# Attention's output projection: remainders of the early tiles ahead of the whole tiles, combinations in that order, first weights' high part sooner

## The reference

```python
def diff_attn(...):
    ...
    o = _rms_f32(o, g_sub) * (1.0 - lambda_init)
    o = o.transpose(0, 2, 1, 3).reshape(B, L, D_V_W).astype(xn.dtype)
    return o @ w_out

def swiglu(xn, w_in, w_out):
    gu = xn @ w_in
    g = gu[..., :FF]
    u = gu[..., FF:]
    return (jax.nn.silu(g) * u) @ w_out

def trunk(...):
    ...
            h = h + diff_attn(...)
        xn = rmsnorm(h, norm_ffn[i])
        h = h + swiglu(xn, ffn_w_in[i], ffn_w_out[i])
    return h[:, N_META:]
```

## Time and profile before

| | |
|---|---|
| median of 3 runs | 1980.11 us (1978.26 to 1980.32) |
| the profiled execution | 1979.85 us |
| its span | 1978.0 us |
| PE busy | 1931.5 us, 98% |
| DVE busy | 1138.6 us, 58% |
| ACT busy | 723.7 us, 37% |
| POOL busy | 1093.0 us, 55% |

### The profile page before, as it was taken

One profiled execution on the slowest core, in us unless ns is written; L12 is line 12 of the kernel. 1 busy time (PEld: TensorE's weight loads), 2 busy tenths in 40 slices (PEclk: granted clock), 3 DMA queues, 4 the chain that ended last, 5 costly groups with the idle time before them and its releaser, 6 DMA issues.

```text
span 1978.0 us, 30306 instructions
## 1 busy us (share of the span) xinstructions
PE 1931.5 (98%) x11129; PEld 1802.3 (91%) x11129; DVE 1138.6 (58%) x1928; ACT 723.7 (37%) x1447; POOL 1093.0 (55%) x1503
## 2 busy tenths in 40 slices
PE   8999999999999999999999999999989999999998
PEld 7898988899999999999978888888888898998997
DVE  7756464777365264266566666666685562562651
ACT  5333333445143142143224444445452340440531
POOL 4532323358596596596622222222467894984973
PEclk9999999999999999999999999999989999999999
DMA  4111111212221221222211111101211222222213
GB/s 158 43 33 40 46 32 33 77 48 59 70 86 55 68 70 56 73 65 71 66 43 33 33 32 32 32 27 38 59 43 57 83 64 71 69 70 59 81 55 95
DMA packets 214920, 114.90 MB, mean 58 GB/s; under 512 B 7011, under 2 KB 213510, under 8 KB 214550
## 3 DMA queue, kind: packets, MB, share of 16 engines
q1 hardware_dynamic: 212816, 112.62, 19.4%
q10 hardware_dynamic: 1990, 0.76, 0.2%
HBM read 108.57 MB, written 4.78 MB: 57 GB/s over the span
## 4 chain that ended last, share of the span: by engine, by line
PE 83%; DVE 6%; POOL 5%; ACT 2%; issue 2%; DMA 2%; ACTq 0%; DVEq 0%; SPq 0%; POOLq 0%
PE ps L625 44%; PE ps L679 25%; POOL wl L555 3%; PE ps L847 3%; PE ps L1008 2%; PE ps L976 2%; POOL wxl L555 2%; PE ps L827 1%; DMA raw<-in_ffn_w_in_dram 1%; PE ps L998 1%; PE ps L910 1%; PE ps L856 0%; DVE raw L1235 0%; PE ps L940 0%; ACT wh L1943 0%
## 5 line engine op out<-in xcount | busy, mean ns | idle before, releaser
L544 POOL CAST wh<-raw 128x256 fp32r<-128x256 f32 x428 | 165.6, 427 | 747.3 <-PE ps L625 710.9
L679 PE MATMUL ps<-sx,wh 128*128 128x400 f32 (+1 forms) x1408 | 368.3, 343 | 7.9 <-POOL wl L555 6.5
L555 POOL TENSOR_TENSOR wl<-raw,wh 128x256 fp32r<-128x256 f32 x352 | 319.2, 936 | 89.7 <-ACT wh L1943 89.4
L548 POOL TENSOR_TENSOR wl<-raw,wh 128x256 fp32r<-128x256 f32 x428 | 333.9, 809 | 10.4
L679 PE MATMUL ps<-sx,wxh 128*128 128x400 f32 (+1 forms) x1056 | 275.8, 342 | 10.5 <-ACT u L1950 8.8
L679 PEld LDWEIGHTS ps<-sx,wh 128*128 128x128 f32 x1408 | 259.2, 189 | 9.0 <-issue 6.8
L679 PE MATMUL ps<-sx,wl 128*128 128x400 f32 (+1 forms) x704 | 241.1, 342 | 0.0
L1943 ACT ACTIVATE wh<-raw 128x512 fp32r<-128x512 f32 x176 | 106.7, 628 | 365.2 <-PE ps L625 239.7
L555 POOL TENSOR_TENSOR wxl<-raw,wxh 128x256 fp32r<-128x256 f32 x220 | 223.7, 1042 | 12.8 <-ACT wxh L1943 12.8
L625 PE MATMUL ps<-xh,wh 128*128 128x400 f32 (+2 forms) x768 | 221.9, 365 | 0.0
L625 PE MATMUL ps<-xl,wh 128*128 128x400 f32 (+2 forms) x768 | 213.2, 351 | 0.0
(11 more groups left out here) (265 smaller groups left out, 3343.5 us busy)
## 6 DMA issues: line engine op xcount, KB each, us to landing
raw<-in_ffn_w_in_dram SPq DMA_DIRECT2D x154, 256.0 KB, 3.0
raw<-in_ffn_w_out_dram SPq DMA_DIRECT2D x48, 384.0 KB, 3.5
raw<-in_m_w_in_dram SPq DMA_DIRECT2D x24, 512.0 KB, 3.8
raw<-in_d_w_in_dram SPq DMA_DIRECT2D x24, 512.0 KB, 3.9
rawx<-in_ffn_w_in_dram SPq DMA_DIRECT2D x22, 256.0 KB, 3.0
raw<-in_m_w_out_dram SPq DMA_DIRECT2D x8, 512.0 KB, 4.1
raw<-in_ffn_w_out_dram SPq DMA_DIRECT2D x16, 256.0 KB, 2.7
wk<-in_x_prompt_dram SPq DMA_DIRECT2D x4, 512.0 KB, 5.8
```

The lines of the kernel that those rows point to most:

```text
L544: ins = pool.tensor_copy(wh[:, slot, c], raw[:, slot, c])
L548: ins = pool.tensor_tensor(wl[:, slot, c], raw[:, slot, c], wh[:, slot, c].bitcast(F32), ALU.subtract)
L555: ins = pool.tensor_tensor(slot_of(j, 1)[:, c], factor(g, j)[:, c], slot_of(j, 0)[:, c].bitcast(F32), ALU.subtract)
L679: mm = pe.matmul(product_bank(g, j, layer), slot_of(j, low_w)[:, k * P:(k + 1) * P], sx[layer][:, k * NPROD + j, low_x, :], start=(j in OP ...
```

## The change

Four things are moved, none added or removed.

- PE: behind the first seven k-steps of `whole(0)` and two of `whole(1)`, the four remainders come first, then what is left of the two whole tiles. The second pair of remainders goes to the banks that the first pair used, and so waits for DVE's adds of the first pair.
- DVE: the adds into h follow that order, and the combinations take the pairs 0, 2, 1, 3 (before 1, 0, 2, 3).
- POOL's splits of LATE[2] and LATE[3] keep their place, but wait for the blocks of the whole tiles, which now count later.
- ACT: the high part of the first weights (product 0) is made in the third combination behind xo, no longer behind its last square.

```diff
-PAIR_ORDER = ((0, 1, 2, 3), (1, 0, 2, 3))
+REST_END, WHOLE_END, LATE_END = OUT1 + 4, OUT1 + 6, OUT1 + 8
+PAIR_ORDER = ((0, 1, 2, 3), (0, 2, 1, 3))
...
             for q in range(2):
-                pool.wait_ge(block_done, WHOLE1 + q + 1)
+                pool.wait_ge(block_done, WHOLE_END + q + 1)
                 split(REST1 + 2 + q, q, REST1 // 2 + 2, wait=False)
...
-            pe.wait_ge(acc_free, WHOLE1)
+            pe.wait_ge(acc_free, OUT1 + 4)
             whole(1, 3, k1=2)
             pe.wait_ge(yl_ready, YL_AT[OUT1])
+            rest(0, 0, 2)
+            rest(0, 1, 1)
+            pe.wait_ge(rest_added, 1)
+            rest(1, 0, 2)
+            pe.wait_ge(acc_free, REST_END + 1)
+            rest(1, 1, 1)
             whole(0, 0, k0=7)
             whole(1, 3, k0=2)
-            rest(0, 0, 2)
-            rest(0, 1, 1)
-            pe.wait_ge(acc_free, WHOLE1 + 1)
-            rest(1, 0, 0)
-            pe.wait_ge(acc_free, WHOLE1 + 2)
-            rest(1, 1, 3)
-            pe.wait_ge(rest_added, 1)
+            pe.wait_ge(rest_added, 2)
             run_block(REST1 + 2, 0, 2, (yh, yl), tokens="packed", free=False)
-            pe.wait_ge(acc_free, REST1 + 1)
+            pe.wait_ge(acc_free, REST_END + 2)
             run_block(REST1 + 3, 1, 1, (yh, yl), tokens="packed", free=False)
...
                 elif at == 0:
-                    add_tile(WHOLE1, LATE[0], 0)
+                    add_rest(0, 2)
...
                 elif at == 0:
-                    add_tile(WHOLE1 + 1, LATE[1], 3)
+                    add_tile(REST_END, EARLY[1], 1)
                 elif last:
-                    add_tile(REST1 + 3, LATE[3], 1)
+                    add_tile(LATE_END + 1, LATE[3], 1)
...
-                if layer == 1 and at < 2:
-                    add_rest(at, *((2, 1), (0, 3))[at])
+                if layer == 1 and at == 0:
+                    add_rest(1, 2)
+                    add_tile(REST_END + 1, EARLY[3], 1)
+                elif layer == 1 and at == 1:
+                    add_tile(WHOLE_END, LATE[0], 0)
+                    add_tile(WHOLE_END + 1, LATE[1], 3)
                 elif layer == 1 and at == 2:
-                    add_tile(REST1 + 2, LATE[2], 2)
+                    add_tile(LATE_END, LATE[2], 2)
                     sum_1(g)
...
                 with_gain(2 * k + 1, xo)
                 if last:
                     weight_high(g, 3, next_n0, g)
+                if layer == 1 and at == KP - 2:
+                    weight_high(g, 0, next_n0, g)
...
                 square(2 * k + 1, 2 * at + 1)
                 if layer == 1 and at == KP - 2:
-                    weight_high(g, 0, next_n0, g)
                     weight_high(g, 1, next_n0, g)
```

More of the change, by code:

```diff
@@ L1198, in add_tile, with add_rest @@
                 add_packed(h[:, m, :], p).then_inc(acc_free, 1)
-            def add_rest(q, p0, p1):
+            def add_rest(q, p):
                 ve.wait_ge(rest_done, q + 1)
-                add_packed(h[:, EARLY[2 * q], :], p0).then_inc(rest_added, 1)
-                add_tile(REST1 + q, EARLY[2 * q + 1], p1)
+                add_packed(h[:, EARLY[2 * q], :], p).then_inc(rest_added, 1)
             def out_blocks(n0, norm, gain_at):
@@ L1935, in weight_high @@
                     if g:
-                        sc.wait_ge(block_done, REST1 + 2)
+                        sc.wait_ge(block_done, REST_END + 2)
                 if j in (0, 3):
@@ L1968, in tile_complete @@
                     else:
-                        n = {LATE[0]: WHOLE1, LATE[1]: WHOLE1 + 1, EARLY[1]: REST1, EARLY[3]: REST1 + 1,
-                             LATE[2]: REST1 + 2, LATE[3]: REST1 + 3}[m]
+                        n = {LATE[0]: WHOLE_END, LATE[1]: WHOLE_END + 1, EARLY[1]: REST_END, EARLY[3]: REST_END + 1,
+                             LATE[2]: LATE_END, LATE[3]: LATE_END + 1}[m]
                         sc.wait_ge(acc_free, n + 1)
```

## The result

The changed kernel takes 1983.67 us (median of 14 runs, 1981.11 to 1985.82), the kernel before, measured beside it, 1980.21 (14 runs). The ratio is 1.0017, 95% interval 1.0009 to 1.0024: slower by 0.17%, inside the 0.2% that I took as the limit of what can be told, but a real 3.5 us where I had forecast 1.3 to 1.5.

A forecast was written before the change was run, and what follows sets the result against it. The prediction took the start of product 2, set by the chain of four combinations on DVE and ACT, as what counts. Its terms summed to +1.5 us there, on a profiled 1979.85: 1981.4 us, range 1977.8 to 1984.6.

The forecast's parts named there:

- the upper bound of the contention: At product 2: every moved POOL subtraction costs one chain operation 0.51 us, only old costs given back; +3.7 us, 1983.6.
- rival B: PE's clock falls in the last wait before product 2, over some 5 us at half deciding; 3 us lost, 1984.4; chance 0.12.
- Start: First combination's start: DVE's first add +1.5 us, but its wait before the next add drops out; net +0.2 us.
- From tx2 to the adds: First combination on DVE, tx2 to adds: POOL is now idle there, 2.65 us becomes 2.10; -0.55 us.
- First tail: First combination, adds to running sum: LATE[2]'s split meets three DVE operations, replacing 0.6 us of old contention; +0.9 us.
- Second combination: LATE[3]'s split meets four DVE operations there, two on the chain (running sum, tx2); +1.0 us.
- Weights' pass: Third combination: first weights' high part made sooner saves 0.57 us, but POOL's split meets two lows; net +0.45 us.
- fourth combination: POOL has one split instead of two there, freeing one of DVE's two lows; -0.5 us.
- Projection 2.5 later: Attention's output projection on PE ends about 2.5 us later, covered since DVE needs the last tile near 1448; no cost.
- My other sign of B: Clock under 1.00 after product 2, with no catching up by 1505, would show the forecast wrong.
- A: POOL's moved splits miss DVE's operations, running in its waits; chain moves -0.5 to -2.5 us, about 1978.4; chance 0.27.
- C: First add's delay not recovered, or a block waits for LATE[2]'s split; first term +1.5 instead of +0.2, 1982.7; chance 0.08.

The follow-up runs named there:

- e6: Kernel before plus four matmuls with unread results in the projection, so that it ends 2.57 us later: 1980.52 us, ratio 1.0005.
- e3: Changed kernel, weights' pass in its old place, LATE[2] split by POOL ahead of the remainders in buffers of its own, LATE[3] into slot 0: 1981.86 us, 1.0013.
- e5: Kernel before with POOL's four subtractions for LATE[3] done twice, same values: 1982.21 us, ratio 1.0010.
- e8: Kernel before with LATE[2] split ahead of the remainders, LATE[3] right behind them, each into own slots, and the weights' pass sooner: 1979.94 us, 0.9995.
- e2: Kernel before with only the first weights' high part moved sooner: 1979.38 us, ratio 0.9998.
- e4: Changed kernel with PE's three waits ahead of product 2 filled with matmuls whose results nobody reads: 1980.88 us, ratio 1.0007.
- e1: Changed kernel with the first weights' high part back in its old place, so the reordering alone: 1983.37 us, ratio 1.0017.
- e7: Kernel before with LATE[2] split ahead of the remainders and LATE[3] from shared raw buffer 1 into slot 0: 1980.46 us, ratio 1.0004.
- e9: Changed kernel with the early splits of e8 for LATE[2] and LATE[3]: 1982.54 us, ratio 1.0010.
- e10: e8 with PE's three waits filled as in e4 (1, 5 and 5 matmuls): 1978.93 us, ratio 0.9994.

## Why the prediction was right, and where its size was not

The sign and "within 0.2%" held. The median lies in the range, near its upper end; it owes that to the room that the range left for the upper bound of the contention and for rival B, since the size itself was 3.5 where I had 1.3 to 1.5. The argument (the chain through DVE and ACT counts, not the projection or product 0) was right: e6 moved the projection's end for nothing, e3 and e5 moved product 2 through POOL alone, and in e8 product 0 started 5 us sooner while product 2 came 1.44 sooner. Term by term, at product 2:

- **Start, +0.2: measured -0.02.** DVE's first two adds came 4.78 and 9.39 us after POOL's first cast, where I had 4.65 and 9.6, and the second without a wait, as said.
- **From tx2 to the adds, -0.55: -0.55.**
- **First tail, +0.9: +1.11.** LATE[2]'s split began where I put it (14.08 after POOL's first cast; I had 14.0) and met three low parts, as I had it, and then the running sum, too (1.52 in place of 0.98).
- **Second combination, +1.0: +2.15. This is the mis-sized term.** I wrote that LATE[3]'s split meets four operations of DVE, two of them on the chain, and that xe "hides behind ACT's high part". I had given the split about 5 us. It lasted 6.98 (1424.34 to 1431.32), because DVE holds POOL up as well: its casts took 2.50 for four in place of 1.43, its subtractions 4.40 in place of 2.83. So it reached eight operations: three at 0.75, five (the running sum, tx2, xe and both low parts) at 1.08 to 1.09. And at 1 us each, DVE has no wait left between them: ACT is ahead, and what had hidden is on the chain.
- **Weights' pass, +0.45: +0.32**, and **fourth combination, -0.5: -0.61.** Their difference, -0.29, agrees with e2's -0.31 by itself.
- **Projection 2.5 later, at nothing: 2.41 later, nothing** (e6).
- Sum: +2.4 in place of +1.5.

Of the second combination's 2.15, 1.95 lie between tx2 and the adds: 4.05 us in place of 2.10. There tx2 costs 0.53 more, xe 0.33, and the two low parts, which my count of the chain left out, 1.09. The running sum, which I had counted, cost nothing: from its start to tx2's it is 1.01 in both kernels (1426.60 to 1427.61 above, 1425.28 to 1426.29 before). The other 0.20 lie ahead of it. The line of before:

```profile
1425.28 0.99 DVE L1252 TENSOR_TENSOR tsum<-tsum,tsq 128x800 f32<-128x800 f32 x1 [0.21 <-ACT tsq L1988]
```

**Rival B came in part.** I priced it at 3 us, to be added if the clock fell in the wait ahead of product 2, and gave it 0.12. It did fall, though not in that wait: it fell within product 0, behind the first of the three waits, and stayed at half through the other two and into product 2, for some 3 us of it, below the 5 us that I had set as deciding. PE lost 1.5 us by it, and 0.7 were still there near 1505, by e4; the next waits took up the rest. My other sign of B, no catching up by 1505, came true for those 0.7. The measured terms plus this are 3.1 at PE near 1505, against 3.5 in the medians; the last 0.4 are within the runs' scatter, and no run parts them. Rivals A and C did not come: POOL's new places met DVE at its densest, and PE waited for no split of LATE[2] or LATE[3].

**The Trainium skill's rule** (SBUF — State Buffer, "Who interferes with whom"), that the port pair which VectorE and GpSimd share is an exclusive lock, would have given +3.5 by my estimate. The measured sum, +2.4, stands between it and mine, and the rows are nearer to the rule than I allowed: from start to start, a DVE operation takes 0.47 alone and a POOL subtraction 0.71; where both are dense, each DVE operation takes 1.01 and each subtraction 1.1, so that a pair takes nearly the sum of the two, 1.18. I had read the price off DVE's side alone (0.51 an operation) and left out that POOL pays as well.

## What to carry to other kernels

When work of one engine slows another, the slowed pair must be laid out in time for both: POOL's split beside a dense DVE is not its old length moved, it took 6.98 us in place of 4.4 undisturbed, and reached operations that a count with its old length left out; a step that "hides" behind a third engine hides only as long as its own engine has waits. Before moving work to a later place, look for an earlier one: the splits, of which one alone cost 2.1 us where it was pushed back (e3 against e1), gave 1.1 when they were pulled ahead (e8, less the pass's 0.3), and that needed a buffer of their own (e8), since a shared one put them right back (e7). A late end on an engine whose next work waits for another chain costs nothing (e6), but splitting one long wait into several moved the clock's fall and its recovery (back at 1450.6 before, near 1458.8 changed), and that can land under the work that counts.

## What the runs showed of the hardware that I had not expected

- DVE and POOL slow each other, DVE by 0.54 an operation and POOL by 0.39 a subtraction where both are dense: from start to start, DVE's 128x384 fp32 operations take 0.47, 0.67 beside POOL's casts of 128x256 and 1.01 beside its subtractions; four casts of POOL go from 1.43 to 2.50, four subtractions from 2.83 to 4.40. DVE's adds from PSUM are not slowed (1.93 to 1.94 for four in every profile).
- The clock need not fall within a wait. It fell 2.5 us into the wait of 6.54 (before), but 1.4 us behind the end of one of 2.82 (changed), 0.3 us behind one of 2.34 (e9) and 0.5 us behind one of 4.63, which passed at full clock (e3). At the wait near 1571, of 2.4 to 2.6 us, it fell, within it or just behind, in six of the profiles and not in the others; where it did, the 372 matmuls behind it took 1.1 to 1.4 us more (rows above). I have no reason for the difference.
- Half clock ahead of the work that counts is free (e8 against e10: 100.41 and 100.38 near 1505), and some 3 us of it under that work cost 0.7 (changed against e4).
